# Retention with its steps overlapped by head, without meetings around it

## The reference, cut to what matters

```python
q = _rope(q, pos, dk, RET_ROPE_THETA) * (dk ** -0.5)      # 8 heads, dk = 64, dv = 128
k = _rope(k, pos, dk, RET_ROPE_THETA)
inner = einsum('bhncd,bhnkd->bhnck', qc, kc) * decay      # decay_h^(i-j), i >= j
o = einsum(inner, vc) + cross part with the state R       # chunks of 128 tokens
mu, var = mean and variance of o over dv
on = (o - mu) * rsqrt(var + GN_EPS) * gn_gain
```

## Time and profile before

| what | before |
|---|---|
| median of the runs | 2896.43 us |
| the profiled execution: its own time, its span | 2897.12 us, 2895.8 us |
| mean granted TensorE clock, share of full speed | 0.952 |
| TensorE matmul busy | 2701.9 us (93%) |
| VectorE, ScalarE, GpSimd busy | 901.5, 931.2, 1279.4 us |
| last matmul of `a.in.vr` to first `cx` addition | 545.12 to 647.41 us |
| TensorE's weight passes L256 | 57% of the chain that ended last |

### The profile page before, as it was taken

How to read it: one execution, slowest core, us unless ns; L and a number is a source line. 1 busy time by engine, 2 the same in 40 slices (tenths; PEclk the granted TensorE clock), 3 DMA queues, 4 the chain that set the end, 5 groups by cost and what they waited for, 6 DMA issues and landing times.

```text
span 2895.8 us, 30322 instructions
## 1 busy us (share of the span) xinstructions
PE 2701.9 (93%) x12126; PEld 2155.6 (74%) x12126; DVE 901.5 (31%) x1515; ACT 931.2 (32%) x1497; POOL 1279.4 (44%) x645
## 2 busy tenths in 40 slices
PE   8999999875999999999999999998978699899998
PEld 7888888643666787888887888887855487788886
DVE  4222111253664212344312455102036323311112
ACT  4233222103554322322223222223255423322221
POOL 4444444304775444444444444444433344444443
PEclk9999999866999999999999999997989799899999
DMA  4222223101000222255422455231310022132221
GB/s 158 96 99 90 96 100 121 66 15 58 1 1 22 88 95 86 93 188 189 161 94 76 164 187 188 93 99 55 99 38 1 15 95 87 51 102 95 93 93 62
DMA packets 87276, 261.50 MB, mean 90 GB/s; under 512 B 10465, under 2 KB 11745, under 8 KB 87137
## 3 DMA queue, kind: packets, MB, share of 16 engines
q1 hardware_dynamic: 83888, 255.46, 25.8%
q10 hardware_dynamic: 3248, 4.12, 0.5%
HBM read 257.44 MB, written 2.10 MB: 90 GB/s over the span
## 4 chain that ended last, share of the span: by engine, by line
PE 67%; DVE 4%; POOL 3%; ACT 2%; issue 1%; DMA 0%; POOLq 0%; DVEq 0%; ACTq 0%
PE ps L256 57%; POOL prob L1447 2%; PE ps L267 1%; PE ps L1246 1%; PE ps L1603 1%; PE ps L1216 1%; PE ps L1203 1%; PE ps L859 0%; PE ps L1204 0%; PE ps L1568 0%; PE ps L292 0%; POOL prob_d L1894 0%; PE ps L1592 0%; ACT hs L444 0%; PE ps L1253 0%
## 5 line engine op out<-in xcount | busy, mean ns | idle before, releaser
L243 POOL TENSOR_TENSOR split_ring<-raw_ring,split_ring 128x1024 fp32r<-128x1024 f32 x416 | 1015.7, 2444 | 1255.8 <-ACT split_ring L236 1255.8
L256 PE MATMUL ps<-hs,split_ring 128*128 128x512 f32 x6240 | 1441.9, 392 | 32.6 <-DVE hs L346 9.2
L256 PEld LDWEIGHTS ps<-hs,split_ring 128*128 128x128 f32 x6240 | 1176.7, 189 | 289.8 <-issue 15.9
L236 ACT ACTIVATE split_ring<-raw_ring 128x1024 fp32r<-128x1024 f32 x416 | 437.2, 1052 | 503.7 <-PE ps L256 488.5
L256 PE MATMUL ps<-ffn_act,split_ring 128*128 128x512 f32 x2112 | 495.4, 397 | 0.0
L256 PEld LDWEIGHTS ps<-ffn_act,split_ring 128*128 128x128 f32 x2112 | 398.1, 188 | 96.7
L527 ACT ACTIVATE ffn_act<-tmp 128x512 fp32r<-128x512 f32 x88 | 55.7, 633 | 405.2 <-DVE tmp L565 405.2
L1447 POOL TENSOR_SCALAR prob<-prob,small 128x512 f32<-128x512 f32 (+3 forms) x128 | 140.4, 1114 | 61.2 <-DVE small L1491 61.2
L565 DVE TENSOR_TENSOR tmp<-ps,tmp 128x512 f32<-128x512 f32 x44 | 30.4, 692 | 311.7 <-PE ps L256 311.7
L256 PE MATMUL ps<-split_ring,hs 128*128 128x512 f32 (+1 forms) x480 | 100.7, 372 | 0.0
L256 PEld LDWEIGHTS ps<-split_ring,hs 128*128 128x128 f32 x480 | 85.4, 188 | 15.0
(11 more groups left out here) (304 smaller groups left out, 2534.8 us busy)
## 6 DMA issues: line engine op xcount, KB each, us to landing
raw_ring<-in_wstream SPq DMA_DIRECT2D x380, 512.0 KB, 3.4
ada_w<-in_w_ada SPq DMA_DIRECT2D x96, 256.0 KB, 3.7
raw_ring<-in_wstream SPq DMA_DIRECT2D x32, 384.0 KB, 3.0
sq<-in_w_ada SPq DMA_DIRECT2D x48, 256.0 KB, 3.6
x<-in_x_t SPq DMA_DIRECT2D x4, 512.0 KB, 6.3
decay<-in_decay ACTq DMA_DIRECT2D x4, 512.0 KB, 3.6
out_t<-x SPq DMA_DIRECT2D x8, 256.0 KB, 2.0
raw_ring<-in_wstream SPq DMA_DIRECT2D x4, 304.0 KB, 2.8
```

Source lines behind the costliest of these rows:

```text
L236: nc.scalar.activation(self.split[:, s, 0, :], self.raw[:, s, :], ACT.Copy).then_inc(self.sem("unit_hi"), 1)
L243: nc.gpsimd.tensor_tensor(self.split[:, s, 1, :], self.raw[:, s, :], self.split[:, s, 0, :].bitcast(F32), ALU.subtract).then_inc(self.sem( ...
L256: mm = self.nc.tensor.matmul(out, lhs, rhs, start=first and j == 0, stop=last and j == 2)
```

## The change

It touches retention alone and the hooks around it.

- The loop goes by head h in nine steps, and each engine's list is shifted: step h does the scores of h, a rotation of one of q, k of the next pair (six in all, in steps 0 to 5), the values of h - 1, and the turn of h - 2.
- Two sets of buffers, by h mod 2: the scores of a head lie in two and a half banks (even heads 0, 1 and half of 2, odd heads the other half of 2, 3 and 4; the last score block waits for the decay of the head before, because they share bank 2), `decayed`, the values' bank (5 or 6), the normalized result, the rotated q and k (by pair), and the decay table, now loaded by head. Rotations and turns share bank 7.
- The rotation of pair 0 moves into `a.in.vr`: TensorE's part behind its unit (1, 1), GpSimd's behind its unit (1, 0), VectorE's in front of its unit (1, 3).
- norm, turn and gain of head 7 move into the compression stage: the norm behind the `cx` additions, the turn behind the last unit, the gain in front of the gelu.
- The meetings in front of and behind retention go, on all four engines.

The moments keep their operations (`dve_ret_moments(h)`: the same lines, by head). Each new function begins by binding `nc, sem, to, at`, which is not shown.

```diff
+RET_SPANS = (SPANS, {2: (5 * T // 2, T - 2 * P), 0: (3 * T, T), 1: (4 * T, T - P), 3: (5 * T - P, P)})
...
+            ("decay", [P, 2, T], F32), ("decayed", [P, 2, 5 * T // 2], F32), ("bn", [P, TB, 6], F32),
+            ("mv", [P, 2, TB, 2], F32), ("o_ret", [P, TB, P], F32))
+        self.o_ret = (o_ret, self.ssq[:, :].rearrange("p (b n) -> p b n", b=TB))
+        self.ret_roped = ((self.tmp[:, 0, :], self.tmp[:, 1, :]), (self.tmp[:, 2, :], self.tmp[:, 3, :]))
+        self.ret_cos = (self.sq[:, 0, :], self.sq[:, 1, :])
...
+            if (name, t, u) == ("a.in.vr", 1, 1):
+                self.pe_ret_first_rope()
...
+            if (name, t, u) == ("a.in.vr", 1, 3):
+                self.tables_here(nc.vector, self.TABLES_A)
+                for z in range(2):
+                    self.dve_ret_rope(0, z, z)
...
+    def ret_span(self, h, kb):
+        off, n = RET_SPANS[h % 2][kb]
+        return self.ps[:, off // T, off % T:off % T + n]
+    def ret_decayed(self, h, kb):
+        off, n = RET_SPANS[h % 2][kb]
+        off -= 5 * T // 2 * (h % 2)
+        return self.sd[:, h % 2, off:off + n]
...
+    def pe_ret_first_rope(self):
+        self.tables_here(nc.tensor, self.TABLES_A)
+        for b, e in enumerate(("tm_act", "tm_dve")):
+            nc.tensor.wait_ge(sem(e), at(e, "a.in.vr", 0, b + 2))
+        for z in range(2):
+            self.pe_ret_rope(0, z, z)
+    def pe_ret_scores(self, h):
+        q, k = self.ret_roped[h // 2 % 2]
+        rows = slice(64 * (h % 2), 64 * (h % 2) + 64)
+        if h % 2 == 0:
+            nc.tensor.wait_ge(sem("roped"), at("roped", "ret", h // 2, 1))
+        if h == 1:
+            nc.tensor.wait_ge(sem("tm_act"), at("tm_act", "a.in.vr", 1, 0))
+        for kb in SPAN_ORDER:
+            if h > 1:
+                nc.tensor.wait_ge(sem("decayed"), at("decayed", h - 2, kb))
+            if kb == 2 and h > 0:
+                nc.tensor.wait_ge(sem("decayed"), at("decayed", h - 1, 2))
+            nc.tensor.matmul(self.ret_span(h, kb), k[rows, kb * P:(kb + 1) * P], q[rows, kb * P:T],
+                             start=True, stop=True).then_inc(sem("ret_scored"), to("ret_scored", h, kb))
+    def pe_ret_values(self, h):
+        if h == 0:
+            for e in ("tm_act", "tm_dve"):
+                nc.tensor.wait_ge(sem(e), at(e, "a.in.vr", 1, 2 + (e == "tm_dve")))
+        if h > 1:
+            nc.tensor.wait_ge(sem("ret_normed"), at("ret_normed", h - 2))
+        nc.tensor.wait_ge(sem("decayed"), at("decayed", h, 2))
+        for qb in range(TB):
+            for kb in range(qb + 1):
+                mm = nc.tensor.matmul(self.ps[:, 5 + h % 2, qb * P:(qb + 1) * P],
+                                      self.ret_decayed(h, kb)[:, (qb - kb) * P:(qb - kb + 1) * P],
+                                      self.vr[:, kb, h * P:(h + 1) * P], start=kb == 0, stop=kb == qb)
+        mm.then_inc(sem("ret_pv"), to("ret_pv", h))
+    def pe_ret_turn(self, h):
+        nc.tensor.wait_ge(sem("ret_normed"), at("ret_normed", h))
+        for b in range(TB):
+            mm = nc.tensor.transpose(self.ps[:, 7, b * P:(b + 1) * P], self.o_ret[h % 2][:, b, :], self.ident[:, :])
+        mm.then_inc(sem("ret_turned"), to("ret_turned", h))
     def pe_retention(self):
+        for h in range(9):
+            i, z = h // 2 + 1, h % 2
+            if h < 8:
+                self.pe_ret_scores(h)
+            if i < 4:
+                if h == 0:
+                    nc.tensor.wait_ge(sem("tm_dve"), at("tm_dve", "a.in.vr", 1, 3))
+                if h in (1, 2):
+                    nc.tensor.wait_ge(sem("rope_sin"), at("rope_sin", "ret", 1, h - 1))
+                if h > 2:
+                    nc.tensor.wait_ge(sem("gained"), at("gained", h - 3))
+                self.pe_ret_rope(i, z)
+            if h > 0:
+                self.pe_ret_values(h - 1)
+            if h > 1:
+                if i < 4:
+                    nc.tensor.wait_ge(sem("rope_sin"), at("rope_sin", "ret", i, z))
+                elif h > 2:
+                    nc.tensor.wait_ge(sem("gained"), at("gained", h - 3))
+                self.pe_ret_turn(h - 2)
+    def pool_ret_cos(self, i, z):
+        if i > 0:
+            nc.gpsimd.wait_ge(sem("roped"), at("roped", "ret", i - 1, z))
+        self.pool_rope(("ret", i, z), self.pr[:, i + 4 * z, :], self.cos_r[:, :], self.ret_cos[z])
+    def pool_ret_first_cos(self):
+        self.tables_here(nc.gpsimd, self.TABLES_A)
+        nc.gpsimd.wait_ge(sem("fm_dve"), at("fm_dve", "a.in.fm", self.plan["a.in.fm"]["n"] - 1, 3))
+        for z in range(2):
+            self.pool_ret_cos(0, z)
     def pool_retention(self):
+        for i in range(1, 4):
             for z in range(2):
+                self.pool_ret_cos(i, z)
+    def act_decay(self, h):
+        self.nc.scalar.dma_start(self.decay[:, h % 2, :], self.dram["decay"][h]).then_inc(
+            self.sem(f"decay_landed{h % 2}"), 16)
+    def act_ret_gained(self, h):
+        nc.scalar.wait_ge(sem("ret_turned"), at("ret_turned", h))
+        tile = h // 2 + 4 * (h % 2)
+        nc.scalar.activation(self.pr[:, tile, :], self.ps[:, 7, :], ACT.Copy, scale=self.vecs[:, 2, tile:tile + 1]
+                             ).then_inc(sem("gained"), to("gained", h))
     def act_retention(self):
+        for h in range(9):
+            if 1 < h + 1 < 8:
+                nc.scalar.wait_ge(sem("decayed"), at("decayed", h - 1, 2))
+                self.act_decay(h + 1)
+            if h > 0:
+                nc.scalar.wait_ge(sem("ret_moments"), at("ret_moments", "inverse", h - 1))
+                st = self.small[:, 12 * ((h - 1) % 2):12 * ((h - 1) % 2) + 12]
+                nc.scalar.activation(st[:, 8:12], st[:, 4:8], ACT.Sqrt).then_inc(sem("ret_rstd"), to("ret_rstd", h - 1))
+            if h > 1:
+                self.act_ret_gained(h - 2)
+    def dve_ret_decay(self, h):
+        nc.vector.wait_ge(sem(f"decay_landed{h % 2}"), 16 * (h // 2 + 1))
+        if h > 1:
+            nc.vector.wait_ge(sem("ret_pv"), at("ret_pv", h - 2))
+        for kb in SPAN_ORDER:
+            n = T - kb * P
+            if kb != 3:
+                nc.vector.wait_ge(sem("ret_scored"), at("ret_scored", h, 3 if kb == 1 else kb))
+            nc.vector.tensor_tensor(self.ret_decayed(h, kb), self.ret_span(h, kb), self.decay[:, h % 2, 0:n],
+                                    ALU.mult).then_inc(sem("decayed"), to("decayed", h, kb))
...
+    def dve_ret_norm(self, h):
+        nc.vector.wait_ge(sem("ret_rstd"), at("ret_rstd", h))
+        if h > 1:
+            nc.vector.wait_ge(sem("ret_turned"), at("ret_turned", h - 2))
+        for b in range(TB):
+            rstd = 12 * (h % 2) + 8 + b
+            ins = nc.vector.tensor_scalar(self.o_ret[h % 2][:, b, :], self.ps[:, 5 + h % 2, b * P:(b + 1) * P],
+                                          self.mv[:, h % 2, b, 0:1], self.small[:, rstd:rstd + 1],
+                                          ALU.subtract, ALU.mult)
+        ins.then_inc(sem("ret_normed"), to("ret_normed", h))
     def dve_retention(self):
+        for h in range(9):
+            if h < 8:
+                self.dve_ret_decay(h)
+            if h < 6:
+                self.dve_ret_rope(h // 2 + 1, h % 2)
+            if h > 1:
+                self.dve_ret_norm(h - 2)
+            if h > 0:
+                self.dve_ret_moments(h - 1)
...
         i.then_inc(sem("cx"), to("cx"))
+        self.dve_ret_norm(7)
         flat = lambda a: a.rearrange("p a b c -> p (a b c)")
...
         for t, u, g in self.units("a.cmp"):
             self.act_split(g + LOOKAHEAD)
         nc.scalar.wait_ge(sem("unit_used"), g + 1)
+        self.act_ret_gained(7)
         for kv in range(2):
             i = nc.scalar.activation(self.hid_rows[:, kv, :], self.ps[0:2 * N_CMP, kv, 0:2 * P], ACT.Gelu_apprx_tanh)
         i.then_inc(sem("hid_rows"), to("hid_rows"))
...
             mm.then_inc(sem("unit_used"), 1)
+        nc.tensor.wait_ge(sem("gained"), at("gained", 6))
+        self.pe_ret_turn(7)
         nc.tensor.wait_ge(sem("hid_rows"), at("hid_rows"))
...
+        nc.tensor.wait_ge(sem("gained"), at("gained", 7))
         self.pe_rope(("cmp",), self.kc_raw[:, :], self.perm_n[:, :], 7, n=N_CMP)
...
         self.pe_tm_project("a.in.vr", 512)
-        self.meet(nc.tensor)
-        self.tables_here(nc.tensor, self.TABLES_A)
         self.pe_retention()
-        self.meet(nc.tensor)
         self.pe_compress()
...
+        self.act_decay(1)
...
-        self.pool_stage("a.in.vr")
-        self.meet(nc.gpsimd)
-        self.tables_here(nc.gpsimd, self.TABLES_A)
+        for t, u, g in self.units("a.in.vr"):
+            self.pool_split(g + LOOKAHEAD)
+            if (t, u) == (1, 0):
+                self.pool_ret_first_cos()
         self.pool_retention()
-        self.meet(nc.gpsimd)
...
```

(48 more changed lines are left out.)

19 lines of the change are left out of this document (14 added, 5 removed).

## The result

The changed kernel takes **2846.9 us** (median of 4, 2846.1 to 2847.8) against 2896.3 (median of 4): a ratio of 0.9829, interval 0.9812 to 0.9846, 49.4 us faster. Forecast was 2850, in 2846 to 2862. The medians leave out two slow executions, 6894.9 us in e6 and 3913.3 us of the kernel before. The table gives the marks of the path; the last row is what is left over.

What follows compares the result with a forecast made beforehand. Retention was taken as one serial chain per pair of heads, half of it hand-overs and low clock. Gain 48.1 - 0.7 = 47.4 us, so 2849.0 on the median, stated as 2850, range 2846 to 2862.

Steps and rivals of the forecast that it cites:

- part 2: Retention's steps laid out one by one: full steps of 6.95 us, first `cx` at 599.3 against 647.4, 48.1 us earlier.
- The loop of five links: In retention's full step: turn, scores, rotation, rotate on VectorE, norm, back to turn; 6.95 us.
- The clock assumption: TensorE, 91% busy in the new retention loop with longest waits of about 0.6 us, was taken to keep clock 1.00.
- Rival B: Low clock stays in retention, steps of 12.0 us: 2889 us; 4% for all, 9% for part (2855 to 2875).
- Rival C: VectorE becomes the bound in retention, a step of 7.7 instead of 6.95 us: 2856 us; 12%.
- part 4: Retention's double buffers cost none; VectorE slowed beside GpSimd's product taken as 0, with a bound of 3.4 us.
- Part 3's thinnest cover: In retention, TensorE's next rotation waits for ScalarE's gain, hidden by 0.25 us; otherwise tenths per step, at most 4 steps.
- Rival D: Attention stage starts with a low clock for longer, slower than before: 2920 us with three pairs; 2%.
- part 5: Tail in compression: norm and turn of head 7 cost 0, its gain in front of the gelu adds 0.7 us.

Runs made afterwards that it cites:

- e6: Changed kernel with four more VectorE operations per head between rotation and norm: 2876.9 us.
- e7: Changed kernel with VectorE's norm(h - 2) in front of its rotation in each step: 2843.7 us.
- e1: Kernel before, with three idle-filling TensorE matmuls behind each pair's rotations and three behind its last values: 2876.3 us.
- e2: Changed kernel, but the decay of head h waits for the values of head h - 1, as with one `decayed` buffer: 2899.2 us.
- e3: Changed kernel with the rotation of pair 0 back at the start of retention on all three engines: 2856.4 us.
- e5: Changed kernel with two more VectorE operations per head between rotation and norm: 2859.3 us.
- e8: Changed kernel with norm(h - 2) before rotation, head 7's gain behind the gelu, and thirteen idle-filling TensorE matmuls before compression: 2843.2 us.
- e4: Changed kernel with both meetings, in front of and behind retention, put back: 2856.9 us.

## Why the prediction was right

- *The chain and its links* (part 2). Measured from TensorE's first scores (547.25), the steps began at 16.0, 22.9, 29.8, 36.7, 41.9 and 47.1, against 16.1, 23.0, 30.0, 36.9, 42.4 and 47.8 forecast; `cx` at 51.7 against 52.3. The loop of five links set the step, and e7 shows it from the other side: with norm out of it, TensorE's own work does.
- *The clock assumption* held: 1.00 over the stage; e1 puts its worth in the old order at 20.4 us. Rival B's 2889 doesn't apply, but its mechanism is what e2, e3 and e6 lost by. The Trainium skill (TensorE: Matmul & The Clock Gate, "A second HAM failure mode: psum-queue depth-cycling") says that short idles between groups of matmuls can make the clock swing. With waits of 0.65 us no swing is seen; the trace of e5, with waits of 1.98 us, has one: scores at 2.42, then 3.67, then 2.42 again.
- *Rival C* falls: GpSimd's product (568.23 to 569.50 in one step) lay beside the norm and the start of the statistics, which took 1.36 and 0.88 us as before (1.35 and 0.88), so part 4's 0 was right. What the rival feared is in the trace elsewhere: in the early rotation, VectorE's add of two SBUF tiles took 2.49 us beside GpSimd's split, and 0.69 alone behind it. It lies in an idle time of VectorE and cost nothing. The timeline:
```profile
535.91 2.39 POOL L249 TENSOR_TENSOR split_ring<-raw_ring,split_ring 128x1024 fp32r<-128x1024 f32 x1 [2.53 <-ACT split_ring L242]
536.35 2.49 DVE L892 TENSOR_TENSOR tmp<-tmp,sq 128x512 f32<-128x512 f32 x1
...
539.48 0.69 DVE L892 TENSOR_TENSOR tmp<-tmp,sq 128x512 f32<-128x512 f32 x1
```
- *Part 3's thinnest cover* held, with 0.61 us instead of 0.25: ScalarE's gain ended at 571.87 (571.20 + 0.67), the rotation that waits for it began at 572.48.
- *Rival D*: NSA was not late; the last row of the table is +0.3.
- **The term that was off** is part 5, the tail: -0.7 forecast, +1.3 measured, 2.0 of the 2.6 us by which the profiled execution beat its sum. The 0.7 itself is there (0.6 between the end of the split and the table load): the gain stands between the last split and the table load, as the timeline of ScalarE and TensorE shows.
```profile
625.93 1.06 ACT L242 ACTIVATE split_ring<-raw_ring 128x1024 fp32r<-128x1024 f32 x1 [0.18 <-DMA raw_ring<-in_wstream]
626.16 0.60 PE L952 MATMUL ps<-ident,ssq 128*128 128x128 f32 x4
626.89 0.67 ACT L1006 ACTIVATE pqr<-ps,vecs 128x512 f32<-128x512 f32 x1
627.58 1.28 ACT L1169 ACT_TABLE_LOAD   x1
```
What I left out is that the work around it got shorter: from the first compression matmul to the end of the last split 15.8 us instead of 16.9, and from the start of the table load to NSA's first rotation 6.4 instead of 7.1. The rows are of the first 4.3 us of the former and of the whole of the latter, in the kernel before:
```profile
659.71:664.00 4.29, 4.29 (x20) 4.29 (x21) 0.18 (x1) 1.06 (x1) 2.39 (x2) 0.50 0.22 76
676.66:683.70 7.04, 3.65 (x22) 2.79 (x22) 1.34 (x7) 3.97 (x6) 3.70 (x3) 0.57 0.61 219
```
and after:
```profile
611.15:615.40 4.25, 4.25 (x25) 4.25 (x26) 0.22 (x1) 1.06 (x1) 2.36 (x2) 0.65 0.23 56
627.50:634.00 6.50, 3.01 (x23) 2.30 (x23) 1.34 (x7) 4.04 (x7) 4.35 (x4) 0.78 0.70 226
```
The clock was higher in both (0.65 for 0.50, 0.78 for 0.57), but only the second goes with it. The way from the table load to NSA's first rotation gets shorter from trace to trace as its clock gets higher: 7.06 at 0.57, 6.62 in e7 at 0.74, 6.39 here, 6.05 in e5 at 0.84. The first does not: e1, whose compression is the code of the kernel before and started at the same 0.50, took 15.8 us, and e7, at 0.63, took 16.4. The first stretch and the last split of e1:
```profile
639.27:643.56 4.29, 4.29 (x20) 4.29 (x21) 0.18 (x1) 1.06 (x1) 2.39 (x2) 0.50 0.23 50
654.00 1.06 ACT L236 ACTIVATE split_ring<-raw_ring 128x1024 fp32r<-128x1024 f32 x1 [1.36 <-DMA raw_ring<-in_wstream]
```
In all these traces the last three splits wait for their loads (1.02, 1.36 and 2.48 us before, 1.61, 2.54 and 0.18 after), and the stretch varies between 15.7 and 16.9 us from one kernel to the next. So 1.1 us of the surplus came from how the loads fell, which nothing in the prediction covers and no run here sets: as far as the forecast goes, it is luck. Only in e8, where most of the wait before compression is filled, does the stretch get clearly shorter (14.7).

The rest of the miss is small: steps 6 and 7 took 5.2 us each where part 2 added up 5.4, which is 0.4 of the 0.6 us in the second row of the table.

## What to carry to other kernels

Lay out one full step of a software pipeline from the old trace's own durations, at the high clock level, and find its loop: here that gave the step to 0.03 us, and moving one link out of the loop gave the next 3 us. Before taking waits away one by one, fill them with idle matmuls (e1): it tells in one run how much of a serial stage is clock and how much is order. Test each buffer that is doubled: of the two tested here, the overlap needed one, and the other was worth nothing.

## What the hardware showed that I had not expected

- The high level outlives a wait: in e3 the scores right behind a 3.00 us wait ran at 2.51, and the next group at 4.63.
- The same wait of 1.98 us before three turns of e5 cost the clock once and not the other times, so a single trace doesn't price such a wait.
- The same VectorE add of two SBUF tiles took 2.49 us beside a GpSimd operation of 2.39 and 0.69 alone.
- A small wait can cost several us of clock, and not where one looks for it: e4's rear meeting, with 1.8 us on the path, cost 7.3 in the median, and the mean granted clock fell from 0.962 to 0.959 in the longest executions.
